# Index products in fours, sample scores in four column groups, the last tile's heads on ScalarE and GpSimd, rounds shifted

## The reference, cut to what matters

```python
s = einsum('bqhe,bse->bqhs', qi, idx_keys)                 # 8 heads of 64
score = einsum('bqhs,bqh->bqs', relu(s), wi) * IDX_SCALE   # weighed sum over the heads
score = where(admissible, score, NEG)
_, idx = top_k(score, topk)                                # 128 of 512 (prompt), 256 of 1025 (sample)
```

## Time and profile before

| | us |
|---|---|
| median of 3 runs | 1205.15 |
| the profiled execution | 1203.8 |
| its span, first to last instruction | 1202.1 |
| TensorE busy | 1157.5 |
| VectorE busy | 890.4 |
| ScalarE busy | 558.9 |
| GpSimd busy | 92.3 |

### The profile page before, as it was taken

How to read it: one execution, slowest core, us unless ns; L and a number is a source line. 1 busy time by engine, 2 the same in 40 slices (tenths; PEclk the granted TensorE clock), 3 DMA queues, 4 the chain that set the end, 5 groups by cost and what they waited for, 6 DMA issues and landing times.

```text
span 1202.1 us, 24762 instructions
## 1 busy us (share of the span) xinstructions
PE 1157.5 (96%) x9294; PEld 1064.4 (89%) x9294; DVE 890.4 (74%) x1759; ACT 558.9 (46%) x1012; POOL 92.3 (8%) x141
## 2 busy tenths in 40 slices
PE   8999988999999999999999999899999999999995
PEld 4959844589999999999999988699999999999995
DVE  2279999857899488597677766768895795795676
ACT  2342158844654353443334566744642443543334
POOL 4425400200000000000510000000000000000000
PEclk9999989999999999999999999999999999999998
DMA  7599480043223324233533221141223223233222
GB/s 214 181 283 291 150 255 23 21 156 108 71 71 107 88 87 140 71 100 112 157 92 104 83 63 42 32 147 63 71 75 120 87 106 95 82 106 105 90 86 71
DMA packets 64048, 132.38 MB, mean 110 GB/s; under 512 B 7835, under 2 KB 36667, under 8 KB 63819
## 3 DMA queue, kind: packets, MB, share of 16 engines
q1 hardware_dynamic: 47899, 115.16, 29.9%
q10 hardware_dynamic: 12688, 9.31, 2.6%
q0 software_dynamic: 3360, 6.56, 1.7%
HBM read 126.46 MB, written 9.79 MB: 113 GB/s over the span
## 4 chain that ended last, share of the span: by engine, by line
PE 78%; DVE 14%; ACT 2%; issue 2%; SPq 2%; DMA 1%; ACTq 0%; DVEq 0%
PE PS L704 34%; PE PS L901 20%; PE PS L736 12%; PE PS L1219 3%; PE PS L1031 2%; PE PS L987 2%; PE PS L972 2%; SPq L479 2%; PE PS L1001 1%; DVE SC L2477 1%; DVE MX L2475 1%; DVE PB L2303 1%; DVE MSK L2486 1%; DMA KVX<-cacheV 1%; DVE YA L2162 1%
## 5 line engine op out<-in xcount | busy, mean ns | idle before, releaser
L704 PE MATMUL PS<-XH,WHI 128*128 128x260 f32 x1088 | 221.5, 285 | 0.7 <-DVE XL L2346 0.7
L704 PE MATMUL PS<-XH,WLO 128*128 128x260 f32 x1088 | 219.1, 283 | 0.0
L704 PE MATMUL PS<-XL,WHI 128*128 128x260 f32 x1088 | 218.8, 283 | 0.0
L704 PEld LDWEIGHTS PS<-XH,WHI 128*128 128x128 f32 x1088 | 167.5, 188 | 5.9 <-issue 4.8
L704 PEld LDWEIGHTS PS<-XH,WLO 128*128 128x128 f32 x1088 | 167.6, 188 | 0.0
L704 PEld LDWEIGHTS PS<-XL,WHI 128*128 128x128 f32 x1088 | 167.3, 188 | 0.0
L1281 ACT ACTIVATE WHI<-WRAW 128x1024 fp32r<-128x1024 f32 x72 | 76.2, 1059 | 178.5 <-PE PS L704 138.5
L1823 DVE TENSOR_TENSOR WLO<-WRAW,WHI 128x1024 fp32r<-128x1024 f32 x64 | 79.2, 1238 | 98.4 <-ACT WHI L1281 98.3
L901 PE MATMUL PS<-HH,RNH 128*128 128x260 f32 x384 | 109.0, 284 | 2.5 <-DVE RNL L1963 2.4
L901 PE MATMUL PS<-HL,RNH 128*128 128x260 f32 x384 | 108.4, 282 | 0.0
L901 PE MATMUL PS<-HH,RNL 128*128 128x260 f32 x384 | 108.3, 282 | 0.0
(11 more groups left out here) (349 smaller groups left out, 2790.0 us busy)
## 6 DMA issues: line engine op xcount, KB each, us to landing
WRAW<-wall SPq DMA_DIRECT2D x168, 512.0 KB, 3.6
bias_skewed<-bias_seq SPq DMA_DIRECT2D x4, 1280.0 KB, 18.3
BT<-bias_skewed ACTq DMA_DIRECT2D x3, 1024.0 KB, 9.0
X<-xT SPq DMA_DIRECT2D x4, 520.0 KB, 6.6
X<-xT SPq DMA_DIRECT2D x1, 2080.0 KB, 11.3
yT<-X SPq DMA_DIRECT2D x8, 260.0 KB
KVB<-cacheK SPq DMA_DIRECT2D x16, 128.0 KB, 3.1
KVX<-cacheK SPq DMA_DIRECT2D x16, 128.0 KB, 3.3
```

The source lines that it names most:

```text
L704: mm = pe.matmul(PS[:, 2 * slot + g, 0:TG], tile, x[:, k, TG * g:TG * g + TG], start=(k == 0 and w is w_hi and x is hi), stop=(k == KT - 1 ...
```

## The change

- Index products: four items ahead of each of the first 6 k tiles of unit 5, instead of three ahead of each of the 8.
- Sample scores: the four products of a span write four different groups of 32 output rows (column groups), each on its own; `SR`, `WB` and `WD` get 128 rows instead of 64, and the sum over the groups is made by `sample_sums`.
- Tile 3's eight items (16 to 23): ScalarE writes the relus to eight places (`SC` and `RS3`, which lies where `UQ`'s units 7 to 13 come later) and does not wait for VectorE. After the sample scores it weighs them in place (`weigh_last_tile`), and GpSimd adds them up (`add_heads`): heads 1 to 3 ahead of unit 8's low part, heads 4 to 7 and the clearing of `QB` behind it. ScalarE's evictions of units 7 and later wait for these adds.
- Sample 3's pages on GpSimd: two behind each of the low parts of units 9 to 12, instead of four ahead of unit 8's and one behind each of the next.
- VectorE: only items 0 to 15, then `sample_queries`, then `low_part(6)`; the scaling of a tile's scores moves to its first round; rounds ahead of `low_part(7)` 5 instead of 10, behind `mask_done` 7 instead of 5, behind the sample's queries 8 instead of 5. Behind the sample's maximum the counts are as before.

```diff
@@ GpSimd
             numbers = page_numbers(pool, 1, V_HALF + V_LATE)
-            pool.wait_ge(ds_mm, 3)
-            nc.gpsimd.memset(QB[:], 0.0).then_inc(z_qb, 1)
-            for pg in range(4):
-                load_page(pool, 3, pg)
+            def add_heads(h0, h1):
+                for h in range(h0, h1):
+                    pool.wait_ge(is_scaled, h + 1)
+                    if h > 1:
+                        pool.wait_ge(is_pool, h - 1)
+                    nc.gpsimd.tensor_tensor(SC[:, 2, :], SC[:, 2, :], RS3[:, h - 1, 0:SEQ], ALU.add
+                                            ).then_inc(is_pool, 1)
+            add_heads(1, 4)
             for u in range(POOL_LO[0], A_OUT):
                 low_part(u, u % 2)
-                if u < POOL_LO[0] + 4:
-                    load_page(pool, 3, 4 + u - POOL_LO[0])
+                if u == POOL_LO[0]:
+                    add_heads(4, IDXH)
+                    nc.gpsimd.memset(QB[:], 0.0).then_inc(z_qb, 1)
+                else:
+                    for pg in range(2 * (u - POOL_LO[0] - 1), 2 * (u - POOL_LO[0])):
+                        if pg < NPG:
+                            load_page(pool, 3, pg)
@@ TensorE
-                        mm = pe.matmul(PSF[0:HD, 2048 + c0:2048 + c1],
-                                       QB[:, HD * c:HD * c + HD], IK[:, c, c0:c1],
-                                       start=(c == 0), stop=(c == 3))
+                        r = slice(32 * c, 32 * c + 32)
+                        mm = pe.matmul(PSF[r, 2048 + c0:2048 + c1], QB[:, r], IK[:, c, c0:c1],
+                                       start=True, stop=True)
...
-                    between = {k: (lambda k=k: index_scores(3 * k, 3 * k + 3))
-                               for k in range(KT)}
+                    between = {k: (lambda k=k: index_scores(4 * k, 4 * k + 4))
+                               for k in range(len(items) // 4)}
@@ ScalarE
+            def weigh_last_tile():
+                act.wait_ge(is_relu, 3 * IDXH)
+                for h in range(IDXH):
+                    x = RS3[:, h - 1, 0:SEQ] if h else SC[:, 2, :]
+                    nc.scalar.activation(x, x, ACT.Copy, scale=NAT[:, 3, HD + h:HD + h + 1]
+                                         ).then_inc(is_scaled, 1)
...
-                        if n >= 2:
+                        if 2 <= n < 2 * IDXH:
                             act.wait_ge(is_acc, n - 1)
+                        if n == 2 * IDXH:
+                            act.wait_ge(toe_out, 16)
+                        to = (RS[:, n % 2, 0:(t + 1) * P] if t < 3 else
+                              RS3[:, h - 1, 0:SEQ] if h else SC[:, 2, :])
...
                     act.dma_start(ORD[:], io["ord"]).then_inc(ord_in, 16)
+                    weigh_last_tile()
...
+                if u >= 7:
+                    act.wait_ge(is_pool, min(u - 6, IDXH - 1))
@@ VectorE
-            for n, (t, h) in enumerate(items):
-                if n == 8:
-                    low_part(6, 0)
-                if n == 16:
-                    sample_queries()
+            for n, (t, h) in enumerate(items[:2 * IDXH]):
...
-            for t in range(1, QT):
+            sample_queries()
+            low_part(6, 0)
+            def finish_scores(t):
+                if t == 3:
+                    dve.wait_ge(is_pool, IDXH - 1)
...
                     if half == 0:
+                        if i == 0:
+                            finish_scores(t)
...
-            prompt_rounds(10)
+            prompt_rounds(5)
             low_part(7, 1)
...
             dve.wait_ge(mask_done, 1)
-            prompt_rounds(5)
+            prompt_rounds(7)
...
             queries(7, 8).then_inc(qb_ready, 1)
-            prompt_rounds(5)
+            prompt_rounds(8)
```

More of the change, by code:

```diff
@@ L202, in one_hot @@
     return (np.arange(NB_)[:, None] == bucket(dist)[None, :]).astype(np.float32)
-C_ID, C_ONE, C_CAUS, C_WIN, C_WD, C_BLK, C_SAM, C_END = 0, 128, 256, 384, 640, 704, 832, 840
+C_ID, C_ONE, C_CAUS, C_WIN, C_WD, C_BLK, C_SAM, C_END = 0, 128, 256, 384, 640, 768, 896, 904
 H_SEQ, H_DEC, H_WIN, H_END = 0, 640, 640 + 1025, 640 + 1025 + 128
@@ L218, in constants @@
     for b in range(DB):
-        c[b, C_WD + 8 * b:C_WD + 8 * b + 8] = 1.0
+        at = C_WD + 32 * (b // 2) + 8 * (b % 2)
+        c[b, at:at + IDXH] = 1.0
         c[NH * b:NH * b + NH, C_SAM + b] = 1.0
@@ L282, in program @@
         IK = place("IK", [P, 4, 1025], at=hw)
-        SR = place("SR", [HD, 1025], at=hw + 4104)
+        SR = place("SR", [P, 1025], at=hw + 4104)
         ORD = place("ORD", [P, 1025], at=hw + 4104)
@@ L332, in program @@
         WK = place("WK", [P, 2, KT, P], F32R, at=kw)
+        RS3 = place("RS3", [P, IDXH - 1, TOK], at=7 * TOK)
         WBT = place("WBT", [P, NH, 512], F32R, at=xw + 16640)
@@ L352, in program @@
         SND = place("SND", [P, 1])
-        WB = place("WB", [HD, P])
+        WB = place("WB", [P, P])
         HSF = place("HSF", [P, 16])
@@ L357, in program @@
         IND = place("IND", [P, 1])
-        WD = place("WD", [DB, HD])
+        WD = place("WD", [DB, P])
         PT = place("PT", [1, 64], I32)
@@ L420, in program @@
         is_mm, is_relu, is_acc = sem("is_mm"), sem("is_relu"), sem("is_acc")
+        is_scaled, is_pool = sem("is_scaled"), sem("is_pool")
         qib_ready, ikn_ready = sem("qib_ready"), sem("ikn_ready")
@@ L1093, in _ @@
                     pe.wait_ge(seq_ev, 1)
-                    pe.transpose(PS[0:HD, 6, 0:DB], WD[:], CST[0:DB, 0:DB]).then_inc(kit_mm, 1)
+                    pe.transpose(PS[:, 6, 0:DB], WD[:], CST[0:DB, 0:DB]).then_inc(kit_mm, 1)
                 if u == 5:
@@ L1657, in _ @@
                         act.wait_ge(is_mm, n + 1)
-                        if n >= 2:
+                        if 2 <= n < 2 * IDXH:
                             act.wait_ge(is_acc, n - 1)
-                        nc.scalar.activation(RS[:, n % 2, 0:(t + 1) * P],
-                                             PS[:, 4 + n % 4, 0:(t + 1) * P], ACT.Relu
+                        if n == 2 * IDXH:
+                            act.wait_ge(toe_out, 16)
+                        to = (RS[:, n % 2, 0:(t + 1) * P] if t < 3 else
+                              RS3[:, h - 1, 0:SEQ] if h else SC[:, 2, :])
+                        nc.scalar.activation(to, PS[:, 4 + n % 4, 0:(t + 1) * P], ACT.Relu
                                              ).then_inc(is_relu, 1)
@@ L1666, in _ @@
                         act.wait_ge(ds_mm, n + 1)
-                        nc.scalar.activation(SR[:, c0:c1], PSF[0:HD, 2048 + c0:2048 + c1],
+                        nc.scalar.activation(SR[:, c0:c1], PSF[:, 2048 + c0:2048 + c1],
                                              ACT.Relu).then_inc(ds_relu, 1)
@@ L1693, in _ @@
                         WB[:].rearrange("p (b h) -> p b h", b=DB),
-                        PS[0:HD, 6, 0:DB].rearrange("p (b o) -> p b o", o=1).broadcast_to(
-                            [HD, DB, NH]), ACT.Copy).then_inc(wb_ev, 1)
+                        PS[:, 6, 0:DB].rearrange("p (b o) -> p b o", o=1).broadcast_to(
+                            [P, DB, NH]), ACT.Copy).then_inc(wb_ev, 1)
                 if u == 3:
@@ L2382, in _ @@
             V.tensor_copy(IDR[:], ident).then_inc(idr_ready, 1)
-            V.tensor_tensor(WD[:].rearrange("p (b h) -> p b h", b=DB),
-                            NAT[0:DB, 4:5, HD:HD + IDXH].broadcast_to([DB, DB, IDXH]),
-                            CST[0:DB, C_WD:C_WD + HD].rearrange("p (b h) -> p b h", b=DB),
+            V.tensor_tensor(WD[:].rearrange("p (b h) -> p b h", h=IDXH),
+                            NAT[0:DB, 4:5, HD:HD + IDXH].broadcast_to([DB, P // IDXH, IDXH]),
+                            CST[0:DB, C_WD:C_WD + P].rearrange("p (b h) -> p b h", h=IDXH),
                             ALU.mult).then_inc(wd_ready, 1)
@@ L2423, in sample_queries @@
                 dve.wait_ge(ev_act, 4)
-                qv = QB[:, 0:320].rearrange("p (c x) -> p c x", x=80)
+                qv = QB[:, 0:P].rearrange("p (c x) -> p c x", x=32)
                 for half in range(2):
```

## The result

| | before | after | ratio, 95% interval |
|---|---|---|---|
| median, us | 1205.15 (5 runs) | 1213.34 (5 runs) | 1.0074, 1.0061 to 1.0087 |
| span of the profiled execution | 1202.1 | 1211.4 | |

The changed kernel is slower by 8.2 us by the medians (8.9 by the ratio, which puts it at 1214.1), where 4.9 were forecast. The direction was the predicted one, and so was the bound (the copies, and the weights behind them). The size was not: the shift d of the mask came out at +2.56 us instead of -0.3. One reason I had not seen at all: ScalarE's page numbers, which made GpSimd a second bound at the same place.

The account below looks back on a forecast made before the run. Bound: the DMA copies and unit 10's weights behind them. d of -0.3 plus VectorE's 5.2 (6.3 rounds, 0.4 scaling, less 1.5 slack) gave +4.9, so 1205.15 became 1210.0 us; range 1203 to 1213.5, the forecast's own 1207 to 1213.

Parts of the forecast that it names:

- shift d of the mask: How far VectorE's mask moves, as units 12 and 13 do; forecast -0.3 us, bounds -3.4 to +3.9.
- What TensorE saves: Step on units 5 and 6: index groups and sample scores save 8.3 us, so unit 7 starts at 90.6, not 98.89.
- 3.1 - 0.9 + 0.6: TensorE's index products in us: 3.1 saved by fours, 0.9 lost to a stall, 0.6 of wait gone.
- What the DMAs do to d: Step: copies begin at 82.2, take 23.7 us, land at 105.9; unit 10 starts at 118.5, so d = -0.3.
- stood out ahead of unit 9 or 10: Claim that the 8.3 us TensorE wins in units 5 and 6 are spent waiting ahead of these units.
- the sum above goes by unit 10 alone: In the DMA step, unit 10's weights alone set d; unit 9's load order matters only for the lower bound.
- Ring order: Each DMA engine consumes a queue's descriptors in order, so unit 9's weights land 1.2 us behind the copies.
- GpSimd: Rival: unit 9's low part waits for adds and memset until 106.5; d = -6.1, in all -0.9, 1204.3 us; chance 0.17.
- What VectorE pays: Step from mask to attention: five more rounds 6.3, scaling 0.4, less 1.5 slack; attention starts d + 5.2 us later.
- So the mask moves exactly as units 12 and 13 do: In the VectorE step: digits have fixed places in TensorE's list and VectorE waits for them, so the mask shifts by d.
- Buys nothing past digit 8: Eight sums and five rounds fewer on VectorE ahead of the digits gain nothing there, since it idles in the digits.
- copies cost what they did before: Rival: late pages crowd unit 10, d = +3.9, in all +9.1 us, 1214.3 us; chance 0.08.

Follow-up runs that it names:

- run 2: The changed kernel with ScalarE's page numbers read in units 2 to 4 instead of ahead of the relu; ratio 1.0076.
- run 4: The changed kernel with ScalarE's page numbers read earlier and low_part(6) back between items 7 and 8; ratio 1.0042.
- run 1: The changed kernel with the sample scores as before, four products one after another in one column group; ratio 1.0092.
- Run 5: The changed kernel with VectorE's rounds back at 10, 5 and 5; ratio 1.0029.
- run 3: The changed kernel with low_part(6) back between items 7 and 8, so the copies are issued earlier; ratio 1.0077.
- run 7: run 6 with the last tile's heads back on VectorE, GpSimd's memset and sample 3's pages back in their old places; ratio 1.0009.
- run 8: run 6 with GpSimd's memset of QB ahead of its adds; ratio 0.9995.
- run 9: run 6 with each of GpSimd's adds of 512 columns cut into two of 256; ratio 0.9979.
- run 12: run 6 once more, unchanged, for a second profile; mask at 136.57 against 134.53, no ratio given.
- run 6: The changed kernel with page numbers read earlier, rounds back at 10, 5 and 5, and low_part(6) back; ratio 0.9981.

## Why the prediction was right and wrong, step by step

- **What TensorE saves.** The terms held: from the first index group to the scores 17.1 us instead of 19.9 (2.8 saved, forecast 3.1 - 0.9 + 0.6), the second group stalled 1.0 (0.9), column groups 5.5. Their sum at unit 7 did not: 97.73, not 90.6. The step of it that failed is the one that passed the 5.5 us of the sample scores on to unit 7 in full: I asked what waits for TensorE's scores, not what lay beside them. ScalarE's page numbers, hidden under 7.49 us of products before, came out, and the clock took 2 us more. With the page numbers moved, run 2 has 90.27. For the end time this mistake alone was worth nothing that can be told (ratio 1.0076 instead of 1.0074); together with the late copies it was worth 3.9 us (run 4).
- **What the DMAs do to d** is the step of the forecast that failed, as the term that was mis-sized. Issue of the copies 82.6 (82.2), landing 108.3 (105.9, bounds 102.8 to 108.9), unit 10's high part 116.55 (114.4), unit 10 at 120.61 (118.5), d = +2.56 (-0.3, bounds -3.4 to +3.9). Copies issued at 82 took 24.2 to 25.7 us in runs 1, 2, 5 and the changed kernel, where I had 23.7. In the changed kernel 7.08 MB moved in these 25.7 us, so 1.8 MB were others' (I counted 1.5), and the rate near alone was about 241 GB/s (255): 5.24 MB at that rate and 1.8 MB at the forecast's 2.1 us each make 25.6 us, an estimate that gives the whole of it. Why the rate was lower stays open; in run 2 as many MB moved in 24.2 us. From their landing to unit 10's high part it took 8.3 (forecast 8.5). And "stood out ahead of unit 9 or 10" had a price I left out: in run 2, where the copies landed at 106.4 and unit 10's high part started at 114.55, both about as forecast, unit 10 was still late at 120.20, since the halved clock behind the wait cost unit 9 1.9 us. So the step "the sum above goes by unit 10 alone" failed as well: with the copies as early as before (run 3) GpSimd held unit 9 at 114.31, and the time stayed.
- **Ring order** (unit 9 1.2 behind the copies): it fits, 1.6 and 1.3 us behind them in the changed kernel and in run 2.
- **GpSimd.** It was a rival on its own and became a second bound at the same time: the adds were 1.3 us each (1.46), but began at 95.8, since the weighing came 7 late; TensorE then waited 1.11 us for GpSimd's part of unit 9. Runs 3 and 4 show it.
- **What VectorE pays.** d + 5.2 was forecast, d + 4.85 measured. Run 5 gives 6.05 for the five rounds from the mask on (6.3), and 0.7 ahead of the mask that I had not seen. "So the mask moves exactly as units 12 and 13 do" is not quite so: unit 13's digit moved from 137.28 to 139.26, 1.98 us, the mask 2.56; the other 0.6 are VectorE's, between the last digit and the mask. Judged by the ratios, 5.4 of the 8.9 us are this step.
- **"Buys nothing past digit 8"** was right for the changed kernel and wrong as a rule: with the other two causes gone, VectorE's 5 us decide (run 7, 3.4 us).
- **The range.** The median, 1213.34, is just inside 1203 to 1213.5 and just outside the forecast's own 1207 to 1213; by the ratio, 1214.1, the change lies above both. The 4.9 us were short by the 2.9 us of d, and in the profiled execution by 1.5 us in layer 2, for which the forecast had no term. The rival "copies cost what they did before" (1214.3, given 0.08) was nearest; it would have deserved more, though its reason (late pages that crowd unit 10) is not what happened: unit 10's weights came 8.3 us behind the copies, not 9.7.

In sum: +2.56 at the mask (copies, weights and GpSimd together), +6.1 rounds, -1.2 slack used, +0.4 in the attention, +1.5 in layer 2 in the profiled execution: 9.3 of span.

## What to carry to other kernels

Before crediting a shorter stage, list what the other engines do during it: what was hidden under it comes out, and loads of registers don't even show as busy. A gain that two late things cover is not found by removing one of them; remove both. And a long wait of TensorE was not paid once here, since the clock behind it was halved: 1.9 to 2.7 us more behind waits of 4 to 6 us. A gain that TensorE only waits out later can therefore cost.

## What the runs showed of the hardware

- One-column VectorE operations with two tensor inputs took up to 1.20 us instead of 0.16, until the GpSimd instruction under way ended; 0.66 beside instructions of half the columns.
- Behind waits of TensorE of 4.94, 6.29, 3.99 and 3.50 us (the changed kernel, runs 2, 7 and 8) the granted clock fell, to 0.50 to 0.60 in the 4 to 6 us behind. Behind shorter ones it was no rule: it fell behind 1.45 us (run 9), 1.54 us (run 4) and 2.13 us (run 12), and stayed at 1.00 behind 2.20 us (run 1).
- The four DRAM to DRAM copies, 5.24 MB, took 24.2 to 28.5 us from the first issue to BT0's load, and nearly alone they moved 237 to 255 GB/s. In two executions of one program (runs 6 and 12) ScalarE got unit 10's weights 2 us apart.
